# A decoder step on one core: earlier loads of the token rows, an earlier norm, and sample states spread over more due time

## The reference, cut to what matters

```
h    = rms_norm(x, g);  proj = h @ w_in                    # 1024 -> 6656 columns
o_a  = stick-breaking attention(qa, ka, va)                # sample: also 4096 cached positions each
o_b  = chunkwise retention(qb, kb, vb)                     # 4 heads, state 128 x 256 each
x    = x + (sigmoid(ga) * (o_a @ w_a_up) + sigmoid(gb) * (gated o_b @ w_b_up)) @ w_out
h2   = rms_norm(x)
x    = x + sum over 8 heads x 16 picked experts of  g * gelu(u[e] . h2) * v[e]
y    = x + sigmoid(rms_norm(x) @ w_ple_gate) * (p @ w_ple)
```

## Time and profile before

| what | value |
|---|---|
| median of 3 runs | 2813.42 us (2803.76 to 2820.01) |
| profiled execution, its own time | 2823.17 us |
| its span | 2821.1 us |
| PE busy | 1869.8 us (66%) |
| DVE busy | 1279.2 us (45%) |
| POOL busy | 1286.1 us (46%) |
| ACT busy | 499.6 us (18%) |
| DMA | 912.52 MB, mean 323 GB/s |
| granted TensorE clock, mean | 0.782 |

### The profile page before, as it was taken

One profiled execution on the slowest core, in us unless ns is written; L12 is line 12 of the kernel. 1 busy time (PEld: TensorE's weight loads), 2 busy tenths in 40 slices (PEclk: granted clock), 3 DMA queues, 4 the chain that ended last, 5 costly groups with the idle time before them and its releaser, 6 DMA issues.

```text
span 2821.1 us, 32996 instructions
## 1 busy us (share of the span) xinstructions
PE 1869.8 (66%) x11154; PEld 988.7 (35%) x11154; DVE 1279.2 (45%) x3210; ACT 499.6 (18%) x1140; POOL 1286.1 (46%) x1172
## 2 busy tenths in 40 slices
PE   6984887898874965776546566566665642384757
PEld 3444343333631522223433334333433310162222
DVE  1124474625344763545344443335343555754461
ACT  2111131201121210111022222222221200101121
POOL 0015245435417471637365433355335467855660
PEclk8997899999986985998767776777765765655778
DMA  5788669889959795999799999999899999999992
GB/s 205 266 261 328 234 227 350 307 313 346 358 180 353 258 403 207 375 374 400 283 362 361 365 334 330 364 374 373 321 332 354 361 402 380 399 365 372 306 374 82
DMA packets 339192, 912.52 MB, mean 323 GB/s; under 512 B 36849, under 2 KB 46226, under 8 KB 338898
## 3 DMA queue, kind: packets, MB, share of 16 engines
q0 software_dynamic: 160512, 580.99, 54.5%
q1 hardware_dynamic: 176258, 323.54, 32.5%
q10 hardware_dynamic: 2256, 5.90, 0.5%
HBM read 894.82 MB, written 15.47 MB: 323 GB/s over the span
## 4 chain that ended last, share of the span: by engine, by line
DMA 25%; PE 18%; POOL 7%; SPq 6%; issue 5%; DVE 3%; ACT 2%; DVEq 0%; ACTq 0%
DMA arena<-in_cache_v_dram 10%; POOL arena L2120 7%; DMA arena<-in_cache_k_dram 5%; SPq L2161 3%; PE ps L2109 3%; SPq L2166 3%; PE ps L790 2%; PE ps L1061 2%; PE ps L466 2%; DMA arena<-in_peer_w_q_dram 2%; PE ps L1106 2%; DMA arena<-in_peer_u_dram,arena 2%; PE ps L861 2%; DMA arena<-in_w_ple_gate_dram 1%; DMA arena<-in_peer_v_dram,arena 1%
## 5 line engine op out<-in xcount | busy, mean ns | idle before, releaser
L2120 POOL DMA_INDIRECT arena<-in_peer_u_dram,arena x544 | 612.8, 1126 | 1035.3 <-PE ps L2109 864.7
L2030 DVE CUSTOM_DVE_ANT_0 arena<-arena 128x1024 f32<-128x1024 f32 x544 | 658.2, 1224 | 552.3 <-DMA arena<-in_peer_u_dram,arena 543.1
L2120 POOL DMA_INDIRECT arena<-in_peer_v_dram,arena x544 | 632.6, 1163 | 246.5 <-issue 159.2
L466 PE MATMUL ps<-arena 128*128 128x512 f32 x1152 | 529.8, 614 | 57.9 <-DMA arena<-in_w_in_dram 20.6
L2109 PE MATMUL ps<-arena 128*32 128x512 f32 x2176 | 333.2, 738 | 143.9 <-DMA arena<-in_peer_v_dram,arena 98.8
L466 PEld LDWEIGHTS ps<-arena 128*128 128x128 f32 x1152 | 219.0, 195 | 352.6 <-issue 270.5
L790 PE MATMUL ps<-arena 128*128 128x128 f32 x1024 | 198.4, 358 | 206.5 <-DMA arena<-in_cache_k_dram 154.2
L790 PEld LDWEIGHTS ps<-arena 128*128 128x128 f32 x1024 | 157.4, 184 | 298.7 <-DMA arena<-in_cache_k_dram 164.4
L1061 PE MATMUL ps<-arena 128*128 128x128 f32 (+2 forms) x1024 | 193.4, 348 | 67.8 <-DMA arena<-in_peer_w_q_dram 67.6
L1061 PEld LDWEIGHTS ps<-arena 128*128 128x128 f32 x1024 | 170.9, 235 | 96.0 <-DMA arena<-in_peer_w_q_dram 73.5
L861 PE MATMUL ps<-arena 128*32 128x512 f32 x512 | 100.9, 871 | 152.5 <-DMA arena<-in_cache_v_dram 152.5
(11 more groups left out here) (217 smaller groups left out, 1740.2 us busy)
## 6 DMA issues: line engine op xcount, KB each, us to landing
arena<-in_w_in_dram SPq DMA_DIRECT2D x156, 512.0 KB, 6.5
arena<-in_cache_k_dram SPq DMA_DIRECT2D x256, 256.0 KB
arena<-in_cache_v_dram SPq DMA_DIRECT2D x256, 256.0 KB
arena<-in_peer_w_q_dram SPq DMA_DIRECT2D x64, 512.0 KB, 9.4
arena<-in_w_out_dram SPq DMA_DIRECT2D x32, 512.0 KB, 5.9
arena<-in_w_b_up_dram SPq DMA_DIRECT2D x24, 512.0 KB, 8.7
arena<-h_for_experts POOLq DMA_DIRECT2D x80, 128.0 KB, 11.8
arena<-in_peer_u_dram,arena POOLq DMA_INDIRECT x544, 9.6
```

The lines of the kernel that those rows point to most:

```text
L466: last = pe.matmul(bank[0:rows(t), :], x[:, c, cs], weight(pe, g.no, name, c), start=(c == 0), stop=(c == nd - 1))
L2030: dve.tensor_tensor_reduce(ring[j], ring[j], HREP[:, g, :], 1.0, 0.0, ALU.mult, ALU.add, A16[:, p, 4 * g + a:4 * g + a + 1]).then_inc(u_us ...
L2120: pool.indirect_dma_start(ring[j], None, table, bass.IndirectOffsetOnAxis(ap=IDX[:, i % 2, 4 * g + a:4 * g + a + 1], axis=0)).then_inc(row ...
```

## The change

Three edits.

1. **Loads.** The rows of group 1 (tiles 1 and 2) are loaded in group 0's part of SP's queue, behind the first half of the gate weights gb0; the rows of group 2 (tile 3 and the sample) in group 1's part, between the weights wq1 and wq3, behind two waits (h2 of the group stored, H2 of tile 2 turned by PE). X0 moves in memory to places that are free then. The waits for the preceding group's stage K, and the load of the first weights of ka that stood ahead of it, go away; the following `load_weights` issues those pieces.
2. **Norm of group 1.** Its due times go from -0.5 .. -0.398 to -0.98 .. -0.92, so that DVE, which calls until(-0.9) ahead of the dots of slot 0, does it before these dots. The rest of group 1 is due from -0.3 on (stage Q; before, from -0.398), and still ends at 5.95.
3. **Sample states.** A request takes four units of stage T and not one. Stage T of group 2 has 43 units and not 19. As group 2 keeps its stretch, 6.02 to 14.2, one unit of 2.5 goes from 0.0368 to 0.0333 slot, stage T goes from 9.454 .. 10.154 to 9.119 .. 10.549, and the other stages of the group are packed about 10% closer.

```diff
-        return dict(hT=f, X0=f + 2048, JUNK0=f + 4096, ...          # group 1
+        return dict(hT=f, X0=f + 8280, JUNK0=f + 4096, ...
-        return dict(hT=f, QT=f + 1280, X0=f + 2560, ...             # group 2
+        return dict(hT=f, QT=f + 1280, X0=f + 2048, ...
-... "T": (2.5, lambda g: RH * len(g.tiles) + 12 * g.sample + 3),
+... "T": (2.5, lambda g: RH * len(g.tiles) + (4 + 4 * DECB) * g.sample + 3),
-PARTS_OF_TIME = [([(0, s) for s in "NQARTGMOK"], -2.0, -1.0), ([(1, s) for s in "NQARTGMOK"], -0.5, 5.95),
+PARTS_OF_TIME = [([(0, s) for s in "NQARTGMOK"], -2.0, -1.0), ([(1, "N")], -0.98, -0.92), ([(1, s) for s in "QARTGMOK"], -0.3, 5.95),
...
-                yield when(q, "T", RH + 2 + b)                      # PE
+                yield when(q, "T", RH + 2 + 4 * b)
-                yield when(q, "T", RH + 2 + DECB + 0.5)             # ACT
+                yield when(q, "T", RH + 2 + 4 * DECB + 0.5)
-                yield when(q, "T", RH + 2 + b + 0.5)                # DVE
+                yield when(q, "T", RH + 2 + 4 * b + 0.5)
...
-                    if q:
-                        load_weights(sp, q, "ka", 0)
-                        drained(q - 1, "K", "pe", "act", "dve")
-                        sp.wait_ge(h2_stored, 16 * g.l0)
-                        load_x(g)
                     if q == 0:
                         load_gain(g)
                     load_weights(sp, q, "gb0", 0)
+                    if q == 0:
+                        load_x(GROUPS[1])
...
                     store_late(g)
+                    if q == 1:
+                        load_weights(sp, q, "wq1")
+                        sp.wait_ge(h2_stored, 16 * g.ln)
+                        wait_full(sp, plan[q, "O"][2][2, 1])
+                        load_x(GROUPS[2])
                     load_weights(sp, q, "wq3")
```

More of the change, by code:

```diff
@@ L181, in memory_of @@
     if q == 1:
-        return dict(hT=f, X0=f + 2048, JUNK0=f + 4096, QT=f + 2048, SQ=f + 3072, QG=f + 4096, QK=f + 5120,
+        return dict(hT=f, X0=f + 8280, JUNK0=f + 4096, QT=f + 2048, SQ=f + 3072, QG=f + 4096, QK=f + 5120,
                     Z=f + 3072, E=f + 6656, oaT=f + 9304,
@@ L188, in memory_of @@
     if q == WITH_SAMPLE:
-        return dict(hT=f, QT=f + 1280, X0=f + 2560, JUNK0=f + 4608, SQ=f + 2560, QG=f + 3584, QK=f + 4608,
+        return dict(hT=f, QT=f + 1280, X0=f + 2048, JUNK0=f + 4608, SQ=f + 2560, QG=f + 3584, QK=f + 4608,
                     Z=f + 2560, E=f + 4608, oaT=f + 7768, QTs=f + 1792, KTs=f + 1920, Vs=f + 2048, PARTS1=f + 6144,
@@ L201 @@
 STAGE_UNITS = {"N": (3.0, lambda g: g.n + 1), "Q": (8.0, lambda g: len(g.order(3)) + 4), "A": (6.0, lambda g: g.steps + 4),
-               "R": (8.0, lambda g: len(g.order(4)) + 4), "T": (2.5, lambda g: RH * len(g.tiles) + 12 * g.sample + 3),
+               "R": (8.0, lambda g: len(g.order(4)) + 4), "T": (2.5, lambda g: RH * len(g.tiles) + (4 + 4 * DECB) * g.sample + 3),
                "G": (8.0, lambda g: len(g.order(2)) + 4), "M": (6.0, lambda g: 8 * len(g.tiles) + 6 * g.sample + 3 if g.n else 5),
```

## The result

The changed kernel takes 2800.14 us (median of 12 runs, 2789.4 to 2814.68), the kernel before 2811.64 us (12 runs, 2800.86 to 2821.02): ratio 0.9959, 95% interval 0.9939 to 0.9978. It is faster by 0.41%, 11.5 us, where 41 us were forecast. Run again beside later kernels it gave 0.9972 (0.9946 to 0.9998). The time lies inside the range, but the size is off by more than three.

What follows compares the result with a forecast made beforehand. PE bounds 282 to 796 us; later PE and DMA are near their limits by turns, with long waits at group handovers. -19.4 - 4.5 - 17 + 0 = -41 us on 2823.2 gives 2782, as median 2772; range 2738 to 2804.

Steps and rivals of the forecast that it cites:

- Part 1, start: Group 1's rows loaded early, norm before slot 0's dots: PE starts Q at 262.9 and not 282.35, 19.4 us earlier.
- what is left is the 19.4 us: PE's work up to weigh(0, 1) stays the same, so group 1 keeps 19.4 us; 30 allowed above, 10 below.
- Rival D: Norm's gain swallowed: DVE delays fourth projection and weights, or slots 1 to 6 wait longer; -10 us, 2803, chance 0.10.
- Its first cause: DVE, with dots from 262.6, holds back the fourth projection and the weights; only some 5 of 19.4 us remain.
- its second: The 20 us come back as longer waits in slots 1 to 6; only some 5 of 19.4 us remain.
- The signs that I had named: Among them: weigh(6, 0) some 24 us earlier than 815.9; under 10 us earlier would mean the swallowed norm gain.
- Part 2: Group 2's rows loaded early: ACT's 5.2 us wait goes, its 6.1 us for top-k stay; -4.5 us (0 to -5).
- Part 3, the chain: Stage T's state requests every 10.2 us; weigh(10, 3) ends 100 us after weigh(9, 0) starts, against 117: -17 us.
- the packing, I take 0: Group 2's other stages about ten per cent closer; slots under stage T give back what these lose: 0, +-10 us.
- From 1401 us on nothing changes: From slot 15 on neither edit changes an instruction's place, so what is won before stays won.

Runs made afterwards that it cites:

- q_dues_kept: Changed kernel with stages Q to K of group 1 due from -0.398 as before, only the norm earlier; 2791.63 us, ratio 0.990 to the kernel before.
- q_from_m033: Changed kernel with stages Q to K of group 1 due from -0.33 and not -0.3; 2784.85 us, ratio 0.9875 to the kernel before.
- states_unpacked: q_dues_kept with group 2's stretch lengthened to 15.09 so its units stay 0.0368 slot, cached attention from 15.14; 2788.12 us, ratio 0.9898.
- no_state_traffic: q_kept_no_states with 12 of 16 state transfers left out, so most of the sample's retention state is not computed; 2766.69 us, ratio 0.9828.
- states_two_units: q_dues_kept with two units a request and not four; 2778.12 us, ratio 0.9876 to the kernel before.
- norm_no_states: Changed kernel without its third edit, one unit for each sample request as before; 2807.43 us, ratio 0.9973 to the kernel before.
- loads_only: Kernel before with only the earlier loads of the rows, all due times and units as before; 2799.82 us, ratio 0.9948.
- q_kept_no_states: q_dues_kept with one unit for each sample request, as before; 2790.38 us, ratio 0.9905 to the kernel before.
- states_only: Kernel before with only the third edit, four units for each sample request; 2812.09 us, ratio 0.9987.
- after_again: Changed kernel, unedited, run again beside a later kernel on the same chip; 2806.74 us, ratio 0.9972 to the kernel before.

## Why the prediction was right or wrong

**Part 1, start: right.** The rows are loaded at 82.6 us (forecast 83), PE starts Q at 260.5 (262.9, in an execution whose stage K ended 2.5 us earlier), weights(0) are at 284.9 (289), weigh(0, 0) at 299.5 (300). DVE did not hold back the fourth projection.

**Part 1, "what is left is the 19.4 us": wrong, and one of two errors of about the same size.** I followed the norm's move to weigh(0, 1) and stopped. The edit also moves the start of Q from -0.398 to -0.3, and with it the last step of stage A over the places around 1.0 where ACT and DVE take up slot 1's and slot 3's expert work. I had put that shift at nothing, without a reason. The lead falls from 18.7 at Q's end to 6.9 at A's. q_dues_kept and q_from_m033 show it from two sides: from N to K of group 1 the lead falls by 15.4 us in the changed kernel, by 1.6 with the old offset, and by 0.6 with 0.03 slot of it. Rival D had the size (some 5 of 19.4 us remain). Its first cause is not what happened, since no dots of DVE were late; of its second, longer waits in slots 1 to 6, one place came true, and a general rise is excluded by q_dues_kept. I gave D 0.10. The signs that I had named missed all this: weigh(6, 0) came 11.8 us earlier (804.10 against 815.86), neither the 24 forecast nor under the 10 that would have meant D. The due times of every step near a whole slot number, which the source gives exactly, should have been worked out as I did for stage T.

**Part 2: right.** The lead rises by 5.4 us over group 2's norm (forecast 4.5), ACT's 6.1 us for the top-k stay, and SP's new waits cost nothing that shows: PE's waits for peer_w_q in group 1 are 6.8 us, and 10.2 before.

**Part 3, the chain: half right.** The mean interval of requests 2 to 7 is (1105.8 - 1060.9) / 5 = 9.0 us (forecast 10.2), though the mean hides 16.5, 8.2, 6.4, 8.1 and 5.8 us, and in the kernel before it was 6.2. Request 2 came at 53 us behind weigh(9, 0) and not 40.5, since the first store left at 35 and not 22: weigh(9, 2) itself had waited for DVE's part of stage T, and DVE for rows of u (10.4 us). Weigh(10, 3) ended at 107 and not 100: -10 us and not -17. The state transfers became slower beside the gathers: stores 9.6 us at the median, and PE's wait for states grew. The Trainium skill ("DMA: Bandwidth & Descriptors", section "Issuing engines are not separate DMA queues") says that DMAs interleave on the same engines whichever engine started them. The trace agrees: the first three stores, beside the gathers, took 10.3, 12.9 and 14.5 us.

**Part 3, "the packing, I take 0": wrong.** The term was the whole balance, not a correction. The states' edit is worth 0 to 4 us, not 17. I had counted -17 in slot 10 and 0 elsewhere, while slots 11 to 13 gave back 12 us. The number of slots being the same is no argument: states_unpacked has slots that are shorter while its background is later. no_state_traffic gives what the waits and the transfers together cost, 23 us.

**"From 1401 us on nothing changes": wrong, for a part of the lead at slots.** From weights(14) to weights(15) the lead rises by 10.7 us, and by 9 to 11 in the other kernels with two or four units a request in the same stretch; in those with one unit it changes by -0.5 to 0.6. In the changed kernel weigh(14, 0) stands ahead of K's last step (1384.80 against 1401.23) and PE then waits 7.4 us for the cached keys where it waited 18.5; that the one brings the other is not shown. How far this edge is kept differs from profile to profile: from K of group 2 to the end of the attention the lead changes by -2.2 us in q_from_m033, by 8.1 in the changed kernel and by 10.0 in states_two_units.

**Sum.** Forecast -19.4 - 4.5 - 17. By the runs: the loads -13.6 by the medians or -14.6 by the ratio (0.9948, parts 1 and 2 without the new order), the early norm with its new offset some +7 (norm_no_states less loads_only), the states 0 to -4. With the offset kept, parts 1 and 2 together are q_kept_no_states: -20.8 by the medians and -26.7 by the ratio, where -23.9 were forecast. So the mechanism of parts 1 and 2 was sized well, and the order that came with it was not: as built, in norm_no_states, they gave -6.0 by the medians or -7.6 by the ratio, 16 to 18 us short, and the states fell 13 to 17 us short. That the time lies in the range owes nothing to the sum: the range was wide enough to take in a loss that the sum did not have.

## What to carry to other kernels

Where two streams are woven by due times, a shift of one stream by a tenth of a slot is an edit of its own (here 0.03 slot decided 15 us of lead at the end of group 1): list which steps cross a place where the other stream's waits stand, on each engine. A shorter period of the foreground proves nothing while the background's own marks have not moved; measure both at a point where both have done the same work. And ask of every lead whether a wait has gone, as in no_state_traffic, where it was kept to the end, or whether work has only been put off, as in states_unpacked, where it was owed.

## What the runs showed of the hardware that I had not expected

A 512 KB state store beside the gathers took 10.3, 12.9 and 14.5 us one after the other (1043.12, 1053.86 and 1067.21 to the loads behind them), while the 3.1 us median of the kernel before belongs to a time in which POOL issued almost nothing (its own first two stores, nearest to the gathers, took 10.3 and 9.1); the loads of the same size took 3.9 to 10.6 us there. So these stores took three to nearly five times as long beside gathers, and this chain did not get shorter by having more room: PE waited longer for states with four units than with one. The median is not steady: in the other kernels with four units it is 4.5 (states_only), 6.7 (q_dues_kept), 7.6 (q_from_m033) and 9.9 us (states_unpacked).

The profiled executions differ by up to 5.8 us at K of group 0, whose due times are the same in all kernels (246.9 in states_two_units, 252.7 in after_again), and the two of the changed kernel by 11.6 us at K of group 2. So a difference of a few us between two profiles, the 4 us of the states' edit among them, shows nothing by itself.
